# First five pieces of the expert matrices requested in the stage before, and the ring of pieces in two buffers

## The reference

```python
def expert_choice_moe(h, router_w, w_gate, w_up, w_down):
    b_, n_tok, d = h.shape
    cap = EC_CAPACITY * n_tok // N_EXPERTS
    affinity = jax.nn.softmax((h @ router_w).astype(F32), axis=-1)
    gate, idx = lax.top_k(jnp.swapaxes(affinity, 1, 2), cap)
    xe = jax.vmap(lambda hb, ib: hb[ib])(h, idx)
    hid = jax.nn.silu(jnp.einsum('becd,edf->becf', xe, w_gate)) * jnp.einsum('becd,edf->becf', xe, w_up)
    ye = jnp.einsum('becf,efd->becd', hid, w_down) * gate[..., None].astype(h.dtype)
    return jax.vmap(lambda ib, yb: jnp.zeros((n_tok, d), yb.dtype).at[ib.reshape(-1)].add(yb.reshape(-1, d)))(idx, ye)
...
        mix_x = merge_branches(deltanet_out(o_dn_x, z_x, dn_norm_g[i]), o_mla_x, gt_x, w_out_a[i], w_out_b[i], w_o[i])
        x_mid = x + mod_x[2] * mix_x
...
        h2 = modulate(x_mid, norm2_g[i], mod_x[3], mod_x[4])
        x = x_mid + mod_x[5] * expert_choice_moe(h2, router_w[i], w_gate[i], w_up[i], w_down[i])
```

## Time and profile before

| | before |
|---|---|
| three runs, us | 4126.62, 4131.1, 4139.81 (median 4131.1) |
| profiled execution, us | 4129.49 |
| its span from first to last instruction, us | 4127.7 |
| PE busy | 3920.5 us, 95% of the span |
| DVE busy | 1676.7 us, 41% |
| read from HBM | 566.15 MB |
| busy share of the DMA engines, 40 slices of the span | 5107611112541110164253111003300416999999 |

### The profile page before, as it was taken

One profiled execution on the slowest core, in us unless ns is written; L12 is line 12 of the kernel. 1 busy time (PEld: TensorE's weight loads), 2 busy tenths in 40 slices (PEclk: granted clock), 3 DMA queues, 4 the chain that ended last, 5 costly groups with the idle time before them and its releaser, 6 DMA issues. The chain is left out here.

```text
span 4127.7 us, 52003 instructions
## 1 busy us (share of the span) xinstructions
PE 3920.5 (95%) x21139; PEld 2417.0 (59%) x21139; DVE 1676.7 (41%) x3136; ACT 857.3 (21%) x1679; POOL 687.2 (17%) x509
## 2 busy tenths in 40 slices
PE   7998899999999999999999999989999999999988
PEld 4565545555448666588845767767656545434333
DVE  2347342233764564443374556543244314111111
ACT  3214320000121333210113333331123201100000
POOL 0003212222420111033242323220003200000000
PEclk9998999999999999999999999999999998999999
DMA  5107611112541110164253111003300416999999
GB/s 178 41 1 274 222 49 62 61 47 102 173 139 57 36 42 26 62 232 171 98 183 71 27 32 29 22 33 116 113 1 1 164 44 252 411 421 422 422 421 364
DMA packets 323236, 580.16 MB, mean 141 GB/s; under 512 B 58700, under 2 KB 189228, under 8 KB 322360
## 3 DMA queue, kind: packets, MB, share of 16 engines
q1 hardware_dynamic: 323000, 576.83, 38.1%
HBM read 566.15 MB, written 10.63 MB: 140 GB/s over the span
## 5 line engine op out<-in xcount | busy, mean ns | idle before, releaser
L3391 PE MATMUL dn_ps<-room,dn_w 128*128 128x512 f32 (+1 forms) x616 | 230.4, 520 | 0.5 <-DVE dn_v_tok L3941 0.3
L972 PE MATMUL ffn_up_ps<-room 128*128 128x384 f32 (+1 forms) x704 | 203.9, 432 | 0.0
L972 PE MATMUL ffn_up_ps<-ffn_up_t,room 128*128 128x384 f32 (+1 forms) x704 | 196.7, 432 | 0.0
L4957 PE MATMUL experts_ps<-experts_ring,experts_xs 128*64 128x512 f32 (+1 forms) x768 | 162.4, 573 | 25.1 <-DMA experts_ring<-in_w_up 25.1
L2679 PE MATMUL hgrn_ps<-room,hgrn_w 128*128 128x512 f32 x372 | 170.4, 593 | 1.4 <-DVE hgrn_v L2934 1.0
L4957 PE MATMUL experts_ps<-experts_ring,room 128*64 128x512 f32 (+1 forms) x768 | 161.0, 570 | 8.7 <-DMA experts_ring<-in_w_up 8.1
L972 PEld LDWEIGHTS ffn_up_ps<-ffn_up_t,room 128*128 128x128 f32 x704 | 133.8, 190 | 55.7
L972 PEld LDWEIGHTS ffn_up_ps<-room 128*128 128x128 f32 x704 | 133.7, 190 | 55.8
L1058 DVE TENSOR_TENSOR room<-ffn_up_ps,room 128x384 f32<-128x384 f32 (+1 forms) x154 | 73.5, 489 | 222.1 <-PE ffn_up_ps L972 220.6
L5051 DVE TENSOR_TENSOR x_sb<-x_sb,experts_ps 128x512 f32<-128x512 f32 x56 | 38.5, 688 | 298.0 <-PE experts_ps L4892 298.0
L3391 PEld LDWEIGHTS dn_ps<-room,dn_w 128*128 128x128 f32 x616 | 112.9, 192 | 76.2 <-issue 66.7
(11 more groups left out here) (699 smaller groups left out, 7355.1 us busy)
## 6 DMA issues: line engine op xcount, KB each, us to landing
experts_ring<-in_w_gate SPq DMA_DIRECT2D x128, 704.0 KB, 14.4
experts_ring<-in_w_up SPq DMA_DIRECT2D x128, 704.0 KB, 17.8
experts_ring<-in_w_down SPq DMA_DIRECT2D x160, 512.0 KB, 12.4
att_wm<-in_mod_w SPq DMA_DIRECT2D x20, 2048.0 KB, 9.1
ffn_w<-in_ffn_w_down SPq DMA_DIRECT2D x37, 1024.0 KB, 4.9
ffn_up_wm<-in_ada_w SPq DMA_DIRECT2D x12, 2048.0 KB, 12.6
ffn_w<-in_ffn_w_up SPq DMA_DIRECT2D x22, 1024.0 KB, 7.6
ffn_front<-in_ffn_w_down SPq DMA_DIRECT2D x18, 1024.0 KB, 4.9
```

Of the source, the lines that this page charges most:

```text
L972: mm = nc.tensor.matmul(result(n, p), lhs[:, k, :], rhs[:, k, :], start=k == 0, stop=k == half - 1)
L3391: mm = nc.tensor.matmul(out, ahead.tile[:, k, :] if k < by_ahead else wt[:, h % 2, piece, k, :], hT[:, k, tok], start=k == 0, stop=k == KD ...
L4957: mm = nc.tensor.matmul(ps[out_rows, 3 * n + c, 0:b - a], xs_now[:, j, at:at + SLOTS], ring[:, w_at + a:w_at + b], start=j == 0, stop=j == ...
```

## The change

The first five pieces (numbers 0 to 4, all of them gate and up) are loaded in SP's queue of the output projection, behind the router's tables. For that, their part of the ring must exist in that stage: it becomes a buffer of its own (`experts_early`, 14080 floats), which lives on to the end, and the rest of the ring (11264 floats) stays in `experts_ring`. The order of places starts in the early buffer, at 11264 of 25344; a piece may not lie across the border of the two buffers. The stage of routing loads pieces 5 to 8 only. The 14 semaphores of the pieces are made at the start of the program. The size of the ring, the pieces, their order and all arithmetic stay.

```diff
@@ -4746,7 +4746,7 @@
             for q, (at, before) in enumerate(places):
-                if before is None:
+                if before is None and q >= EARLY:
                     load(sp, q)
...
 RING_FLOATS = 9 * 2 * EXPERT_FF
+EARLY = 5
+EARLY_AT = RING_FLOATS - EARLY * 2 * EXPERT_FF
 PIECES = 14
...
-    places, at = [], 0
+    places, at = [], EARLY_AT
     for q, size in enumerate(sizes):
+        if at < EARLY_AT < at + size:
+            at = EARLY_AT
         if at + size > RING_FLOATS:
             at = 0
         before = [p for p in range(q) if places[p][0] < at + size and at < places[p][0] + sizes[p]]
         places.append((at, before[-1] if before else None))
         at += size
     return places
+
+
+def ring_part(ring, at, n):
+
+    low, early = ring
+    return early[:, at - EARLY_AT:at - EARLY_AT + n] if at >= EARLY_AT else low[:, at:at + n]
...
-    closing(nc, "wo", hT, KD, wo_jobs, x, mix, hT, ident, (mod, 2, None), (I["norm2_g_2"][0], mod, 3, 4), CTX_TILES, ahead=wo, then=router.load, router=router)
-    return router
+    early = stack.enter_context(nc.sbuf_tensor("experts_early", [P, RING_FLOATS - EARLY_AT], F32, side="right"))
+    load = expert_loads((None, early), piece_in, I["w_gate_2"][0], I["w_up_2"][0], I["w_down_2"][0], expert_places())
+
+    def router_and_experts(sp):
+        router.load(sp)
+        for q in range(EARLY):
+            load(sp, q)
+
+    closing(nc, "wo", hT, KD, wo_jobs, x, mix, hT, ident, (mod, 2, None), (I["norm2_g_2"][0], mod, 3, 4), CTX_TILES, ahead=wo, then=router_and_experts, router=router)
+    return router, early
...
-        ring = sb("experts_ring", RING_FLOATS)
+        ring = (sb("experts_ring", EARLY_AT), early)
```

More of the change, by code:

```diff
@@ L4956, in _ @@
                             w_at = places[pair * pieces + 2 * j + side][0] + n * F
-                            mm = nc.tensor.matmul(ps[out_rows, 3 * n + c, 0:b - a], xs_now[:, j, at:at + SLOTS], ring[:, w_at + a:w_at + b],
+                            mm = nc.tensor.matmul(ps[out_rows, 3 * n + c, 0:b - a], xs_now[:, j, at:at + SLOTS], ring_part(ring, w_at + a, b - a),
                                                   start=j == 0, stop=j == KD - 1)
@@ L4987, in _ @@
                                 w_at = places[pair * pieces + 2 * j + side][0] + (f - a) * 512
-                                mm = nc.tensor.matmul(ps[out_rows, 6 + half, :], hidT[:, f, out_rows], ring[:, w_at:w_at + 512], start=f == 0, stop=f == FT - 1)
+                                mm = nc.tensor.matmul(ps[out_rows, 6 + half, :], hidT[:, f, out_rows], ring_part(ring, w_at, 512), start=f == 0, stop=f == FT - 1)
                         if b == FT:
@@ L5006, in _ @@
                                 w_at = places[pair * pieces + 2 * j + side][0] + at
-                                mm = nc.tensor.matmul(ps[out_rows, 6 + half, :], hidT[:, f, out_rows], ring[:, w_at:w_at + 512],
+                                mm = nc.tensor.matmul(ps[out_rows, 6 + half, :], hidT[:, f, out_rows], ring_part(ring, w_at, 512),
                                                       start=f == 0, stop=f == FT - 1)
@@ L5157, in load @@
                 src = w[e].rearrange("(k p) f -> p k f", p=P)[:, j, :]
-                sp.dma_start(ring[:, at + n * F:at + (n + 1) * F], src).then_inc(landed, 16)
+                sp.dma_start(ring_part(ring, at + n * F, F), src).then_inc(landed, 16)
         else:
@@ L5162, in load @@
             if half is not None:
-                to = ring[:, at:at + (b - a) * 512].rearrange("p (f d) -> p f d", d=512)
+                to = ring_part(ring, at, (b - a) * 512).rearrange("p (f d) -> p f d", d=512)
                 for f0, f1 in ((a, a + 2), (a + 2, b)):
@@ L5169, in load, with second_block @@
                 part = src[:, a + n, :] if b - a == 2 else src[:, a, n * width:(n + 1) * width]
-                sp.dma_start(ring[:, at + n * width:at + (n + 1) * width], part).then_inc(landed, 16)
+                sp.dma_start(ring_part(ring, at + n * width, width), part).then_inc(landed, 16)
     return load
-def second_block(nc, I, x, hT, mix, cst, ident, mod, first, loaded, dn):
+def second_block(nc, I, x, hT, mix, cst, ident, mod, first, loaded, dn, piece_in, stack):
     proj = nc.dram_tensor("proj2", (N_TOK, S_ALL), F32).ap()
@@ L5202, in second_block, with mixture @@
     branches(nc, "mix2", hT, I["w_out_a_2"][0], I["w_out_b_2"][0], delta_out, proj, I["dn_norm_g_2"][0], mix, spare, ident, mix2, wo.load)
-    closing(nc, "wo", hT, KD, wo_jobs, x, mix, hT, ident, (mod, 2, None), (I["norm2_g_2"][0], mod, 3, 4), CTX_TILES, ahead=wo, then=router.load, router=router)
-    return router
-def mixture(nc, I, out, x, room, mix, mod, first, router):
+    early = stack.enter_context(nc.sbuf_tensor("experts_early", [P, RING_FLOATS - EARLY_AT], F32, side="right"))
[6 more added lines that the diff above has]
+    return router, early
+def mixture(nc, I, out, x, room, mix, mod, first, router, early, piece_in):
     n_slots = EXPERTS * SLOTS
@@ L5217, in mixture @@
         slot = sb("slot", lat, EXPERTS)[:, :, :]
-        ring = sb("experts_ring", RING_FLOATS)
+        ring = (sb("experts_ring", EARLY_AT), early)
         hidT = sb("experts_hidT", EXPERT_FF // P, P)
         xs_odd = sb("experts_xs", KD, 2 * P)
-        piece_in = [stack.enter_context(nc.semaphore(f"experts_piece_in{n}")) for n in range(PIECES)]
         places = expert_places()
@@ L5245, in program @@
         nc.semaphore("first_odd_in") as odd_in,
+        contextlib.ExitStack() as stack,
     ):
@@ L5248, in program @@
         mix = room[:, TILES * D:].rearrange("p (m d) -> p m d", d=D)
+        piece_in = [stack.enter_context(nc.semaphore(f"experts_piece_in{n}")) for n in range(PIECES)]
         with nc.sbuf_tensor("cst", [P, N_TABLES, P], F32) as cst:
             dn = first_block(nc, I, x, hT, mix, cst, cst[:, IDENT, :], sc, mod2, first, (even_in, odd_in))
-            router = second_block(nc, I, x, hT, mix, cst, cst[:, IDENT, :], mod2, first, (even_in, odd_in), dn)
-        mixture(nc, I, out, x, room, mix, mod2, first, router)
+            router, early = second_block(nc, I, x, hT, mix, cst, cst[:, IDENT, :], mod2, first, (even_in, odd_in), dn, piece_in, stack)
+        mixture(nc, I, out, x, room, mix, mod2, first, router, early, piece_in)
 INPUTS = (
```

## The result

| | before | after |
|---|---|---|
| median of 22 runs each, us | 4133.98 (4126.62 to 4139.89) | 4141.82 (4133.94 to 4148.99) |
| ratio of the times, 95% interval | | 1.0017 (1.0012 to 1.0023) |
| profiled execution, us | 4129.49 | 4145.48 |
| its span, us | 4127.7 | 4143.7 |
| first release to the end of the span, us | 651.0 | 658.3 |

The change costs 0.17% (0.12 to 0.23%), 7 us by the ratio, where +1.3 us was forecast: no measurable change by the bound of 0.3%, but the median of 4141.82 us lies outside the range of 4122 to 4141. Of the 9.4 us between it and the forecast of 4132.4 (4131.1 + 1.3), 2.9 us are the base, whose median was 4131.1 over three runs and is 4133.98 over 22; the other 6.5 are what the change costs over the forecast (7.8 us between the medians).

The account below looks back on a forecast made before the run. Transfers bound the experts' end: first release, plus bytes behind it over the rate, plus time the queue runs dry. Terms 0.0 + 1.2 + 0.1 = +1.3 us on a median of 4131.1 gave about 4132, range 4122 to 4141.

Parts of the forecast that it names:

- no measurable change: Whole kernel: time changes by no more than about 0.3%, 12 us, which a measurement can't tell from nothing; chance 0.87.
- the lead: Start of the experts: ring full some 18 us sooner, but first release stays at 3476.67, so gain 0.0 us.
- The faster rival: Experts' transfers: all move up by the five early pieces, end 17.1 us sooner, 4114 (0.41%); chance 0.06.
- the other two: Rivals: queue runs dry at every pair's up-to-down turn, 4143 to 4155, chance 0.05; early bytes delay the logits, chance 0.02.
- The paragraph on the fixed part of a DMA: At the first release: the skill's 2.0 us instead of 1.5 us would start the empty queue 0.5 us later.
- piece 27: Pair 0's turn from up to down: its load waits for the first down pieces, queue dry longer, +1.2 us.
- The rest: Semaphore clearing under 0.1 us each, matmul reading another buffer 0, ten issues moved 0; counted as 0.1 us.
- the same 263.8 MB at the same rate: Experts, behind the first release: the remaining 215 pieces still flow at 421 GB/s, taking 626.6 us.
- if stretches after 3550 fall under 415 GB/s: Saturated experts' stretch: one of the signs that would show the prediction wrong; before, none there fell under 421 GB/s.
- 22.7 us: End of the kernel: from the matmuls awaiting the last transfer, at 4105.13, to the span's end; unchanged.

Follow-up runs that it names:

- e4: Changed kernel with its first five pieces loaded in routing again, two buffers and new places kept; ratio 1.0020 to the kernel before.
- e3: Kernel before with the changed kernel's order of places in its one buffer, no early load; ratio 1.0001 to the kernel before.
- e5: Changed kernel with 56 unused floats so the early buffer starts at byte 172800, a multiple of 256; ratio 1.0009 to the kernel before.
- e2: Kernel before with 8 unused floats ahead of its ring, which then starts at byte 111392; ratio 1.0040 to the kernel before.
- e6: Kernel before with 16 unused floats ahead of its ring, which then starts at byte 111424; one run, 4152.18 us.
- e7: Kernel before with 32 unused floats ahead of its ring, which then starts at byte 111488; one run, 4147.20 us.
- e8: Kernel before with 64 unused floats ahead of its ring, which then starts at byte 111616; one run, 4135.98 us.
- e1: Changed kernel with 8 unused floats so the early buffer starts at byte 172992, a multiple of 64; ratio 1.0016 to the kernel before.
- e9: Changed kernel with three early pieces instead of five, early buffer at byte 195328, a multiple of 256; ratio 1.0003 to the kernel before.
- e10: Kernel before with a Silu on an unused tile at the start of the experts' stage, loading its table early; ratio 1.0001 to the kernel before.
- e11: e9 and e10 together: three early pieces at a multiple of 256, and Silu's table loaded ahead; ratio 1.0009 to the kernel before.

## Why the prediction was right and wrong

**Right: the lead is worth nothing.** The ring was full at the first release, the release didn't move against TensorE's start (4.96 us after it, 4.97 before), the engines stood still in between, and with the early loads undone (e4) the time is the same. The faster rival is refuted. So are the other two: after 3557 the rate is even (418, 418, 419, 417 in the slices), the lowest stretch of 6 us between 72 and 600 us behind the release has 402 GB/s, so no later pair's turn empties the queue by a step, and the early bytes were in 3.5 us ahead of the first logits.

The paragraph on the fixed part of a DMA compared unlike things. The Trainium skill ("DMA: Bandwidth & Descriptors", Anatomy of one DMA) gives it for DMAs that GpSimd issues, and puts most of it behind the last byte, while the 1.5 us worked out from the earlier trace rows lie ahead of the bytes of DMAs that SP issued. The sum doesn't use it.

**Right in bytes, not shown in time: piece 27.** +1.2 us forecast. e3 has it alone, at +1.24 us of bytes at the turn. That everything behind is then as much later isn't borne out: in e3 the last up step comes 0.4 us sooner than before, and in e5, which has the same places and loses 361 against 389 GB/s (1.9 us of bytes) at the turn, it comes at the same 609.3. How the later pairs make good for it is open.

**Wrong: the step "The rest", where the second buffer was costed at 0, and with it "the same 263.8 MB at the same rate".** I asked what TensorE reads from the new buffer and not where the DMA engines write it. At its start of 224 bytes past a multiple of 256 a packet takes 218.0 ns instead of 215.3, +1.25%; 14080 of 25344 floats of the ring lie there, so 0.7% of 626.6 us, 4.3 us. The measured rates are near that: the long stretch alone loses 528 x (1 - 418.4/421.7), 4.1 us, and it holds 84% of those bytes, which makes 4.9 us for all. With the start at a multiple of 256, e5, the rate is back at 422 GB/s and the stage at 651.1 us. The prediction's own test was "if stretches after 3550 fall under 415 GB/s"; at 418 it wouldn't have fired, and yet 4.1 us in 528 (0.8%) of a stage that is all transfer are over three times the sum that I forecast.

**The account.** Of the 7.3 us in the profiled stage 7.0 are there at the last up step (616.3 against 609.3), and some 4.3 (by the packets) to 4.9 (by the rates) are the start of the early buffer; that such a start costs this is shown by e2, e6 and e7 against e8, and by e5. The other 2 to 3 us are not isolated. e4 and e1 have such a rest too. Two things are common to these three kernels: piece 27 waits for the first step of down, and that step runs at half clock, so that the queue runs empty; e4 has 332 GB/s at the turn, e1 337, after 342, and e5, with piece 27 but at the full clock, 361. But each of the two alone costs nothing at the last up step: piece 27 in e3 and e5 (608.9 and 609.3), the half clock in e8 (608.6) and in e6 against e2 (621.1 and 621.2). Whether both together do, or the start costs more than its packets show, no run tells: e5 differs from after in the start and in the half clock at once. Single profiles also scatter: e9, e10 and e11 reach the last up step 2 us sooner than the kernel before, and their ratios are 1.0001 to 1.0009.

The end of the changed kernel differs as well. Its last wait for a transfer is the one ahead of the last up step, which then runs at half clock:

```profile
4081.16 20.44 DMA experts_early<-in_w_up
4101.61 0.14 issue
4101.74 6.64 PE experts_ps L4957 x24
```

6.64 us instead of the 4.94 of the step ahead of it. From there to the end TensorE waits for no transfer, where the kernel before waits once more, at 4105.13. So the prediction's 22.7 us "which the change doesn't touch" are no longer what follows the last wait: TensorE sets the last 42 us. e4 is the same; e1, without the half clock there, waits 1.43 us for a down piece instead. So this step costs at most its 1.7 us, and in part takes the place of a wait.

By the ratios of the times, e5 is some 3 us below after, which the intervals don't tell from nothing, and 3.7 us (0 to 7.4) above before. What shows the price of the start in the time itself is e2, at 1.0040 (1.0026 to 1.0053).

**Open.** The 2 to 3 us above. What sets off the half clock at pair 0's turn in 5 of 13 profiles, and what moves the stages ahead of the first release by up to 10 us between executions. Also whether the half clock there is commoner in after than in before, which would be a share of the difference in the medians; no run counted it. e5 in more executions, with and without the half clock, would tell the two causes apart.

## What to carry to other kernels

An early load is worth nothing as long as the buffer is full when its first piece is released: compare the time at which the buffer fills with the time of the first release before moving loads. In this kernel a buffer that transfers of 5632 bytes a partition fill at the full rate had to begin at a multiple of 256 bytes in its partition to lose nothing. A change that splits or moves such a buffer should be read for its new start, not only for its order. After such a change look at the GB/s of the longest saturated stretch first: 418 for 422 at the same busy share was the clue.

## What the runs showed of the hardware that was not expected

- Writes into the on-chip memory from HBM in packets of 5632 bytes depend on the start in the partition: 215.2 ns at a multiple of 256 bytes, 219.5 ns at 32, 64 and 128 past one, 217.5 at 192 and 218.0 at 224 past one. The last two come from kernels where the other buffer was aligned, so they may not compare directly with the first three.
- The DMA share doesn't show this loss: 1.02 at 413, 418 and 422 GB/s.
- A transfer into an empty queue: SP issues piece 27 at 3541.57, and the stretch of 3542 to 3545 is already at 205 GB/s.
- TensorE's granted clock can fall to half for one step of 16 matmuls behind a wait of 2.7 us: in 5 of 11 profiles with that wait, without a pattern in the code, and in neither of the two without it, which are too few to tell. It falls behind waits for transfers too, and not behind each: behind 2.02 us the last up step took 6.64 us in after and 4.95 in e1; behind 2.12 us the last waiting down step took 5.35 us in e2, and behind 2.02 us 3.65 in e7.
